# Engine orders, smaller GpSimd pieces and the sample rows' softmax moved inside attention, in a two-layer hybrid decoder step

## The reference

```python
u, q, k, v, q_idx, k_idx, w_idx, gate_a, gate_b = split(h @ w_in)
y_ssm, s_re, s_im = s5_mixer(u, h0_re, h0_im, ...)   # complex diagonal scan, 32 groups of 16 channels, 64 states
y_a = (y_ssm @ glu_w) * sigmoid(y_ssm @ glu_v)
# prompt: scores = sum_h relu(q_idx . k_idx) * w_idx, causal; the 128 best keys of each query; softmax over them
# sample: the same scores over 2048 cached keys and the new one; the 256 best slots are gathered:
phys = page_table[pidx // PAGE_SIZE]; slot = pidx % PAGE_SIZE
k_sel = cache_k[layer, phys, slot]; v_sel = cache_v[layer, phys, slot]      # (8, 256, 8 heads, 64)
p = softmax(q . k_sel * HEAD_DIM ** -0.5)
attn = p @ v_sel
y_b = attn @ w_branch_attn
mixed = (sigmoid(gate_a) * y_a + sigmoid(gate_b) * y_b) @ w_out
```

## Time and profile before

| | |
|---|---|
| Time, median of 3 runs | 3385.96 us (3383.24 to 3388.85) |
| Profiled execution, its own time | 3386.58 us |
| Its span | 3384.9 us |
| TensorE (PE) busy | 2947.8 us, 87% |
| Weight loads (PEld) busy | 2734.4 us, 81% |
| VectorE (DVE) busy | 1684.5 us, 50% |
| ScalarE (ACT) busy | 1246.4 us, 37% |
| GpSimd (POOL) busy | 335.9 us, 10% |

### The profile page before, as it was taken

How to read it: one execution, slowest core, us unless ns; L and a number is a source line. 1 busy time by engine, 2 the same in 40 slices (tenths; PEclk the granted TensorE clock), 3 DMA queues, 4 the chain that set the end, 5 groups by cost and what they waited for, 6 DMA issues and landing times. The chain is left out here.

```text
span 3384.9 us, 56303 instructions
## 1 busy us (share of the span) xinstructions
PE 2947.8 (87%) x21826; PEld 2734.4 (81%) x21826; DVE 1684.5 (50%) x3238; ACT 1246.4 (37%) x2062; POOL 335.9 (10%) x319
## 2 busy tenths in 40 slices
PE   6999996688988869999769999966888897799996
PEld 4899996688766668999749999966887675699996
DVE  5542445765677444323454424467657674433234
ACT  5542334344343234322155423343443432342221
POOL 2000001123022210000010000010230321100000
PEclk8999997899888989999879999978989899799998
DMA  7443434111122422232164434331211234232321
GB/s 234 125 148 101 151 109 127 44 51 51 44 70 85 123 77 75 84 101 75 39 213 146 143 102 154 103 124 32 57 51 48 63 97 122 63 87 81 106 76 49
DMA packets 452489, 324.09 MB, mean 96 GB/s; under 512 B 25113, under 2 KB 403345, under 8 KB 451546
## 3 DMA queue, kind: packets, MB, share of 16 engines
q1 hardware_dynamic: 446906, 296.60, 29.5%
q0 software_dynamic: 5408, 25.17, 2.3%
HBM read 310.48 MB, written 11.24 MB: 95 GB/s over the span
## 5 line engine op out<-in xcount | busy, mean ns | idle before, releaser
L1128 PE MATMUL PS<-h_hi,w_hi 128*128 128x260 f32 (+1 forms) x4000 | 846.8, 294 | 46.6 <-DVE h_lo L1722 34.7
L1128 PE MATMUL PS<-h_lo,w_hi 128*128 128x260 f32 (+1 forms) x4000 | 819.0, 287 | 0.0
L1654 DVE TENSOR_TENSOR lo_apart<-stage,w_hi 128x1024 fp32r<-128x1024 f32 (+2 forms) x448 | 495.7, 1142 | 466.0 <-ACT w_hi L763 458.2
L1128 PEld LDWEIGHTS PS<-h_hi,w_hi 128*128 128x128 f32 (+1 forms) x4000 | 633.0, 193 | 99.6 <-issue 72.4
L1128 PEld LDWEIGHTS PS<-h_lo,w_hi 128*128 128x128 f32 (+1 forms) x4000 | 630.5, 193 | 0.0
L1128 PE MATMUL PS<-h_hi,lo_apart 128*128 128x260 f32 x2816 | 569.3, 284 | 0.0
L763 ACT ACTIVATE w_hi<-stage 128x1024 fp32r<-128x1024 f32 (+3 forms) x586 | 541.3, 955 | 52.4 <-DMA stage<-in_mod_w 30.4
L1128 PEld LDWEIGHTS PS<-h_hi,lo_apart 128*128 128x128 f32 x2816 | 437.4, 190 | 0.0
L1128 PE MATMUL PS<-hid_lo,w_hi 128*128 128x260 f32 x1408 | 285.9, 285 | 0.0
L1128 PE MATMUL PS<-hid_hi,lo_apart 128*128 128x260 f32 x1408 | 285.6, 284 | 0.0
L1128 PE MATMUL PS<-hid_hi,w_hi 128*128 128x260 f32 x1408 | 285.6, 284 | 0.0
(11 more groups left out here) (407 smaller groups left out, 4048.7 us busy)
## 6 DMA issues: line engine op xcount, KB each, us to landing
stage<-in_ffn_in SPq DMA_DIRECT2D x176, 512.0 KB, 4.0
stage<-in_mod_w SPq DMA_DIRECT2D x144, 512.0 KB, 4.7
stage<-in_w_in SPq DMA_DIRECT2D x72, 512.0 KB, 3.8
stage<-in_ffn_out SPq DMA_DIRECT2D x64, 384.0 KB, 3.7
stage<-in_ffn_out SPq DMA_DIRECT2D x64, 320.0 KB, 3.4
stage<-in_w_out SPq DMA_DIRECT2D x16, 512.0 KB, 4.1
x_hold<-xT SPq DMA_DIRECT2D x2, 2080.0 KB, 6.5
xT<-x_hold SPq DMA_DIRECT2D x2, 2080.0 KB, 8.0
```

The lines of the kernel that those rows point to most:

```text
L1128: return nc.tensor.matmul(out, lhsT, rhs, start=start, stop=stop)
L1654: nc.vector.tensor_tensor(lows(ch)[:, ch.slot, 0:ch.elems], stage[:, ch.slot, 0:ch.elems], w_hi[:, ch.slot, 0:ch.elems].bitcast(FP32), ALU ...
```

## The change

Seven edits, none of which changes what is computed:

1. **VectorE's order in the ki and u tiles.** `rotations(5, 6)` goes behind `samples_operands`, `new_keys` follows at once, and the last level of rotations is cut into two halves (`last_rotation(0)`, `(1)`), done after the scores of page groups 0 and 2. `held_inputs` goes after group 5, the zeroing of `BX`, `BXl` and `plain_inputs` after 7, `powered_inputs(0, r)` after 11 and 13.
2. **Gate tiles.** `powered_inputs(t + 1, 0)` and `(t + 1, 1)` go from the first tile of each four to the third, the first ahead of `skipped(t)`, the second behind the part of the selection that stands there.
3. **ScalarE before attention.** The last split of the `v` tiles goes ahead of the 16 copies scaled by `owner`; the copies of the values out of PSUM (`values_out`) go behind the first exponentials.
4. **Rank distances** in four operations of 4 slots each.
5. **One ring of 4 buffers** for gathered keys and values (instead of 3 and 8). `key_products(b)` in units 15 to 22, one each unit; the sum of a unit goes ahead of the next product. SP loads queries 4 to 7 ahead of the last two pairs of `glu` weights. `Exd` and `own_head` lie elsewhere, and `Exd` is zeroed before the gathers.
6. **Softmax and value products of the samples** in units 23 to 30, all in one PSUM half (`PS[:, 2, 1]`); what stays behind unit 31 is the head mask and the eight small products.
7. **Output projection** unrolled; its first tile waits for the blocks of `mx_lo` one by one.

The diff, cut to its core:

```diff
@@ buffers
-    K_BUFS = 3
+    KV_BUFS = 4
-    kv = [over(f"kv{i}", [P, 2, DA], at) for i, at in enumerate((
-        kv0_at, l_at, l_at + ROWS, bias_at, bias_at + ROWS, lg_at, lg_at + ROWS, rv_at))]
+    kv = [over(f"kv{i}", [P, 2, DA], at) for i, at in enumerate((kv0_at, rv_at, l_at, l_at + ROWS))]
-    Exd = over("Exd", [P, (2 * DEC + 2) * DEC * H], score_at)
-    own_head = over("own_head", [DEC * H, DA], kout_at)
+    Exd = over("Exd", [P, (2 * DEC + 2) * DEC * H], kout_at)
+    own_head = over("own_head", [DEC * H, DA], rl_at)
-    sample_beside = {16 + 2 * b: b for b in range(DEC)}
+    sample_beside = {15 + b: b for b in range(DEC)}
+    weighed = 24
+    first_value = weighed + 2
+    values_beside = {first_value: (0,), first_value + 1: (1, 2), first_value + 2: (3, 4), first_value + 3: (5, 6), first_value + 4: (7,)}
...
@@ SyncE
+                query(4)
                 glu_pair(6)
-                query(4)
                 query(5)
-                glu_pair(7)
                 query(6)
                 query(7)
+                glu_pair(7)
...
@@ ScalarE
                 key_rows(3)
+                split(chunk('v', 5))
                 act.wait_ge(ranks_ready, 1)
                 for v in range(2):
...
                 last.then_inc(rv_ready, 1)
-                split(chunk('v', 5))
                 act.wait_ge(fin_ready, 4)
...
+                def sample_weights():
+                    act.wait_ge(sm_ready, 1)
+                    nc.scalar.activation(Ex[:], Ex[:], ACT.Exp, scale=HD ** -0.5)
+                    nc.scalar.activation(b64[:, 3, :], b64[:, 3, :], ACT.Exp, scale=HD ** -0.5).then_inc(es_done, 1)
+
                 exps(0)
+                values_out()
                 for n in range(NU):
...
+                    if n == weighed + 1:
+                        sample_weights()
...
@@ TensorE
+                def new_values():
+                    pe.wait_ge(pall_ready, 1)
+                    mm(sample_out, pnd[:].rearrange("p b h -> p (b h)"), v_s[0:DEC, :], start=True, stop=False)
+
+                def sample_values(b):
+                    pe.wait_ge(k_in[b % KV_BUFS], arrived(DEC + b))
+                    for c in range(2):
+                        last = mm(sample_out, Exd[:, (2 * b + c) * DEC * H:(2 * b + c + 1) * DEC * H], kv[b % KV_BUFS][:, c, :],
+                                  start=False, stop=(b == DEC - 1 and c == 1))
+                    last.then_inc(vg_used, 1)
...
+                    if n == weighed:
+                        pe.wait_ge(mx_ready, 1)
+                        turn(PS[0:DEC * H, 2, 1, 192:192 + P], b64[:, 0, :], P).then_inc(mx_turned, 1)
+                    if n in values_beside:
+                        if n == first_value:
+                            new_values()
+                        for b in values_beside[n]:
+                            sample_values(b)
                     fill(n)
+                    if n == weighed:
+                        pe.wait_ge(mx_ready, 2)
+                        mm(PS[:, 2, 1, 320:384], ones[0:DEC * H, :], dg64[:]).then_inc(mx_spread, 1)
+                    if n == weighed + 1:
+                        pe.wait_ge(es_ready, 1)
+                        mm(PS[:, 2, 1, 384:448], ones[:], b64[:, 4, :]).then_inc(es_summed, 1)
...
-                evicted('wo')
-                pe.wait_ge(mx_lo_ready, KD)
-                with pe.Fori(0, 2) as i:
+                for i in range(2):
                     for u in range(4):
-                        pe.wait_ge(ev_a, i * 4 + (evicts_a['wo'] + u - 3))
-                        tile(u, [(chunk('wo', u, i, 4), 0, KD, P)], (mx_hi, mx_lo))
+                        if i:
+                            pe.wait_ge(ev_a, 4 + (evicts_a['wo'] + u - 3))
+                        else:
+                            pe.wait_ge(ev_d, evicts_d['br'] + 5 + u)
+                        tile(u, [(chunk('wo', u, i, 4), 0, KD, P)], (mx_hi, mx_lo), h_waits=None if i or u else 0,
+                             blocks_ready=mx_lo_ready)
...
@@ VectorE
+                def last_rotation(r):
+                    n = NCH // 2
+                    cn, sn = (pw[:, 2 + levels - 1, q].unsqueeze(2).to_broadcast([P, GP, n]) for q in ((0, 1), (1, 0))[r])
+                    x1, x2 = ecos[:, 0], ecos[:, 1]
+                    own(nc.vector.tensor_tensor(x1, E[:, 0, :, 0:n], cn, ALU.mult))
+                    tt(x2, E[:, 1, :, 0:n], sn, ALU.mult)
+                    tt(E[:, r, :, n:2 * n], x1, x2, (ALU.subtract, ALU.add)[r])
...
-                rotations(5, 6)
                 for u in range(4):
                     split(chunk('u', u + 2))
                     if u == 0:
                         dve.wait_ge(ev_a, evicts_a['ki'] + 1)
                         samples_operands()
-                        rotations(6, 7)
-                        held_inputs()
-                    if u == 1:
+                        rotations(5, 6)
                         new_keys()
...
                     for g in scored_beside(u):
                         weighted(g)
-                    if u == 2:
-                        powered_inputs(0, 0)
-                        powered_inputs(0, 1)
+                        if g in (0, 2):
+                            last_rotation(g // 2)
+                        if g == 5:
+                            held_inputs()
...
                     if g % 4 == 0:
                         products(t)
-                        if t < 3:
-                            powered_inputs(t + 1, 0)
                     if g % 4 == 1:
                         scans(t)
                     if g % 4 == 2:
+                        if t < 3:
+                            powered_inputs(t + 1, 0)
                         skipped(t)
...
+                    if g % 4 == 2 and t < 3:
+                        powered_inputs(t + 1, 1)
...
+                def sample_maxima():
+                    wide = Lg[:].rearrange("p b c h -> p (b c) h")
+                    tt(wide, wide, vb[:, 0].unsqueeze(2).to_broadcast([P, 2 * DEC, H]), ALU.add)
+                    dve.wait_ge(nl_spread, 1)
+                    own(nc.vector.tensor_tensor(bh(1), PS[:, 2, 1, 128:128 + DEC * H].rearrange("p (b h) -> p b h", h=H),
+                                                vb[:, 1, 0:DEC].unsqueeze(2).to_broadcast([P, DEC, H]), ALU.add))
+                    nc.vector.tensor_tensor(bh(0), Lg[:, :, 0], Lg[:, :, 1], ALU.max).then_inc(mx_ready, 1)
...
+                def weights_scaled():
+                    dve.wait_ge(es_summed, 1)
+                    tt(b64[:, 5], PS[:, 2, 1, 384:448], b64[:, 3], ALU.add)
+                    own.step(nc.vector.reciprocal(b64[:, 5], b64[:, 5]))
+                    dve.wait_ge(exd_zeroed, 1)
...
                 for n in range(TT * H):
+                    if n == weighed:
+                        sample_maxima()
+                    if n == weighed + 1:
+                        sample_lowered()
+                    if n == weighed + 2:
+                        weights_scaled()
...
+                    if n == weighed:
+                        maxima_spread()
+                    if n == weighed + 1:
+                        weights_added()
...
-                dve.wait_ge(vg_used, 1)
+                dve.wait_ge(vg_used, DEC)
...
@@ GpSimd
-                    pool.tensor_tensor(oh[q % 2][:], iota_f[:].unsqueeze(1).to_broadcast([P, n, P]),
-                                       eq[:, q * n:(q + 1) * n].unsqueeze(2).to_broadcast([P, n, P]), ALU.subtract)\
-                        .then_inc(distances_ready, 1)
+                    for s in range(0, n, 4):
+                        last = pool.tensor_tensor(oh[q % 2][:, s:s + 4, :], iota_f[:].unsqueeze(1).to_broadcast([P, 4, P]),
+                                                  eq[:, q * n + s:q * n + s + 4].unsqueeze(2).to_broadcast([P, 4, P]), ALU.subtract)
+                    last.then_inc(distances_ready, 1)
...
                 for b in range(DEC):
-                    if b == K_BUFS:
-                        pool.wait_ge(att_lo, TT)
-                        pool.wait_ge(mx_ready, 1)
-                        pool.memset(Exd[:], 0.0).then_inc(exd_zeroed, 1)
-                    gather('cache_v', b, kv[b], v_in[b])
+                    if b < KV_BUFS:
+                        pool.wait_ge(kg_used, DEC - KV_BUFS + b + 1)
+                    else:
+                        pool.wait_ge(vg_used, b - KV_BUFS + 1)
+                    gather('cache_v', b, kv[b % KV_BUFS], k_in[b % KV_BUFS])
```

151 lines of the change are left out of this document (66 added, 85 removed).

## The result

| | before | after |
|---|---|---|
| Median | 3383.26 us (3383.17 to 3388.85, 5 runs) | 3364.74 us (3364.13 to 3369.92, 5 runs) |
| Ratio to before | | 0.9944, interval 0.9930 to 0.9959 |
| Span of the profiled execution | 3384.9 us | 3362.2 us |

The change gains 0.56% of the time. I had forecast 54.6 us, and it gives about 20. In the experiments the kernel before ran again beside each group, at medians of 3381.1 to 3385.7 us.

What follows compares the result with a forecast made beforehand. TensorE, 87% busy, was taken as the bound, so only its standstills and low clock could matter. Seven parts summed to -27.3 us a layer, -54.6 for two: 3386.6 to 3332 us, own range 3316 to 3348, with rivals 3303 to 3366.

Steps and rivals of the forecast that it cites:

- u tiles: Input projection and page scores: TensorE's two waits shrink, less a late page group 8; -12.3 us a layer, bounds -8 and -13.6.
- Gate tiles: Powered inputs in the third tile, where VectorE is late already, cost +8.2 us a layer, bounds 0 and +11.
- I add 1.2 us for that: Gate tiles: allowance for VectorE's powered inputs running beside GpSimd's two state products of 3.43 us; part of +3.3 us.
- Start of attention: First turn_scaled waits for the last value copy, not the scaled diagonal: -3.1 us a layer, bounds 0 and -4.
- Rank distances: Units 4 to 9: with smaller GpSimd pieces VectorE is held 0.5 us on average; -10 us a layer, bounds -5 and -12.
- Key products: Units 15 to 23: VectorE's products and sums fall on units with top-k rounds; +3.2 us a layer, bounds 0 and +9.
- SP's queries and glu loads change places, and each stays a unit ahead of its use: Key-product units: the reordered loads still arrive in time; no cost was given for them.
- Softmax and values: Tail work moves into units 23 to 30, saving 24.6 us but lengthening units: -5.9 us a layer, bounds -2 and -10.
- rival (e): Softmax chain over three units stalls TensorE by what the tail had, so that move gives 0: 3344 us, chance 0.06.
- Output projection: Tile 0 starts early and waits only for the last mx_lo block: -7.4 us a layer, bounds -5 and -8.
- (a): Attention units: rank distances give only 5 us and key products cost 8; +10 a layer, 3352 us, chance 0.2.
- (d): Slower than before: VectorE-bound units 18 to 30 drop TensorE's clock; +41 us a layer, 3414 us, chance 0.04.

Runs made afterwards that it cites:

- gates_query: The changed kernel with the powered inputs back in the first gate tile of each four and query 5 loaded ahead of glu pair 6: 3318.41 us, ratio 0.9806.
- gates_only: The kernel before with only the powered inputs moved from the first to the third gate tile of each four: 3413.89 us, ratio 1.0086.
- query_first: The changed kernel with SyncE's load of query 5 ahead of glu pair 6 instead of behind it: 3350.20 us, ratio 0.9899.

## Why the prediction was wrong, step by step

1. **u tiles: right.** -11.5 for -12.3, and alone 0.77% of the time. Following the scoring group by group held: its waits are 1.53, 2.80 and 2.83 us where before had 2.09 and 2.83, one short wait more as I had said of group 8.
2. **Gate tiles: the sign right, the size wrong.** +19.2 where the edit acts, for 8.2: 4.5, 7.9 and 6.8 us for t = 0, 1 and 2, for 1.6, 3.3 and 3.3. Two steps failed. The larger is a term that the sum does not have: I priced the longer waits at their own length, and the clock fell behind them (an average of 0.87 for 0.94 over the three quarters), which is 8.2 of the 19.2 us. The other is "I add 1.2 us for that". I had the products of together 3.43 us and the operations beside them in my rows, and charged an average. But the first of these operations starts right behind a split, with GpSimd's product already begun, and each of the two multiplications is held, once for each state product (1.42 and 1.41 us for 0.35): 2.1 us, not 1.2, ahead of `kk`. My 3.3 us were also less than the terms named for them (1.65, 1.65 and 1.2 make 4.5), with no word on what covers the rest; the idle time that came was 4.1 us. In all three quarters it was 11.0 us for my 8.2. No run shows a source for the upper bound of +11, which was my estimate; what the runs showed in its place is 11.0 us of idle time and 8.2 at the lower clock.
3. **Start of attention: right**, -2.5 for -3.1.
4. **Rank distances: mechanism right, size off.** -7.6 for -10. The mis-sized terms are the hold (0.5 to 0.9 us, not 0.5), and unit 9, which stayed at the low clock (0.53, 6.39 us; I had 4.9) behind a wait of 2.69 us. The wait alone does not decide that: in layer 1 of gates_query unit 9 takes 3.89 us behind a wait of 2.71.
5. **Key products: own work right, two things missed.** Against gates_only, units 14 to 23 of query_first (neither has the lateness) take 49.5 us for 46.1: +3.5 for my 3.2 (+2.1 against before, whose units 16 and 17 take 14.6 us for 13.2 in gates_only). The failed step is "SP's queries and glu loads change places, and each stays a unit ahead of its use": query 5 did not, 2.6 to 5.3 us. I had checked who uses a query, not what it is queued behind on SyncE. The lateness, 4 us, no row of before that I read pointed to.
6. **Softmax and values: right.** -6.9 for -5.9. Units 26 to 30 grew by 14.11 us (35.67 for 21.56), and I had 14.6 from 0.43 us a product; units 24 and 25 by 4.2, and I had 3.7. So rival (e) did not come.
7. **Output projection: right**, -7.3 for -7.4.

Four of seven sizes were right and all signs; the sum failed since the one large loss was taken at less than half, and two smaller terms erred the same way. By luck the last quarter gave some 4 us a layer of it back. Of the rivals (a) came nearest, with 3352 us from parts 4 and 5; but held operations (1.42 us for 0.35), and the clock behind them (0.87 for 0.94), decided the gate tiles, which (a) left alone. One more sum does not come out: the bounds of the seven parts, taken as independent (the root of the sum of their squares), give nearly 10 us a layer and not 8. (d) did not come: in layer 0 units 18 to 23 and 26 to 30 ran at a clock of 1.00 (the rows from 1067.99 and 1112.36), though in layer 1 units 18 to 23 averaged 0.89. Without the gate edit and with the query early the change would have given what I forecast and more (0.9806 against my 0.984).
